# A mixture-of-experts kernel: each expert's result added to the output by two scatters of 512 columns instead of one of 1024

## The chip, the core and the metric

One core of a Trainium2 chip. The time is the device time of one launch in microseconds (us), as the median of several runs. Engines are called by the profile's names: PE (TensorE), PEld (its weight loads), DVE (VectorE), ACT (ScalarE), POOL (GpSimd), SP (SyncE, which here only issues loads and stores; its rows read SPq).

## What is computed

One block of a model, in float32, for 512 tokens of width 1024: a normalisation, three mixing branches (dilated attention, a gated recurrence, attention on a memory), an output projection, and then a mixture of experts with 64 experts, of which each token goes to 8. The change lies in the last part:

```python
D_MODEL = 1024
SEQ = 512
N_EXPERTS = 64
TOP_K = 8
EXPERT_HIDDEN = 256

def swiglu(t, w_up, w_down):
    gate, up = split_cols(t @ w_up, (w_down.shape[0], w_down.shape[0]))
    return (jax.nn.silu(gate) * up) @ w_down

# in routed_experts, for each block of rows of one expert e:
        tok = tok_of_slot[slots]
        y = swiglu(u_pad[tok], w_exp_up[e], w_exp_down[e])
        return acc.at[tok].add(y.astype(jnp.float32) * w_of_slot[slots][:, None]), None

# in reference:
        x = x + y.reshape(B, S, D)
```

An expert's weights are 1024 x 512 (up) and 256 x 1024 (down) floats: 3 MB an expert, 192 MB in all. On average 512 x 8 / 64 = 64 tokens go to an expert.

## The kernel before

The front part (projection, branches, router, shared expert) takes the first 600 us and isn't touched. Then the experts run one after another, 64 times the same work on up to 96 rows (`ROWS`). The program is written by hand for each engine, with semaphores between them; nothing is scheduled by a tool, so the order of each engine's instructions is the order of the code.

For expert e:

- SP loads three blocks of 1 MB (two of up, one of down, lines 450 and 452) into 12 buffers, that is, up to four experts ahead. A load waits only for PE to have used the block that lay in its buffer (`block_used`).
- POOL gathers the expert's rows of `u_dram` by the token numbers in `index` (`gather`, line 512), into one of two buffers; 96 descriptors, of which those that hold no token (4096 and above) are skipped by the bounds check. It waits until PE has turned the rows of expert e - 2 (`gT_done`).
- PE turns the rows (`transpose_tokens`, L1786), ACT and DVE split them into a high and a low part (`gatheredT`, L550 and L1346), and so they do with each weight block (ACT `high`, L550, DVE `low`, L1339).
- PE does `up` (24 matmuls of 512 columns) and, after DVE's gate (L1353, L1356) and another turn (L1807), the down product (12 matmuls) into two banks, one for each half of the 1024 columns (all in L1436).
- ACT copies the two banks into `y_out` (`result`), one of two buffers, and raises `y_ready` after the second copy.
- POOL adds the rows of `y_out` to the output in DRAM with an accumulating indirect DMA (`scatter`, line 520). It waits for `y_ready` and for the whole scatter of the expert before (`added`), since two experts may add to the same token's row.

On POOL the order is gather(e + 3), scatter(e), gather(e + 4), scatter(e + 1) and so on; its queue is in order, so that a gather stands behind the scatter before it. On PE it is, for expert n: turn of the hidden rows of n, `up` of n + 1, turn of the gathered rows of n + 2, down of n. Line 501 is `wait_pass`, the helper that waits; `index_ready` comes from DVE (`read_deal`, lines 1333 and 1334), once. A second pass for experts with over 96 tokens is in the program and isn't taken here: the trace has 64 gathers and 64 scatters.

Of the kernel before, what the change touches and what calls it, by code (L numbers as in the profile page):

```python
# [20 lines left out]
U32 = mybir.dt.uint32  # L21
ALU = mybir.AluOpType
# [4 lines left out]
D, T, M = 1024, 512, 256  # L27
# [6 lines left out]
E, FH = 64, 256  # L34
# [8 lines left out]
ROWS = 96  # L43
# [7 lines left out]
NO_TOKEN = 4096.0  # L51
# [50 lines left out]
def build(nc, io, out, const, u_dram, table_dram, debug=None):  # L102
    ctx = ExitStack()
    with ctx:
        def sem(name):
            return ctx.enter_context(nc.semaphore(name))
# [7 lines left out]
        def at(offset, *shape):  # L114
            return view(arena[:, offset:offset + int(np.prod(shape))], *shape)

        def take(*shape):
            offset = top[0]
            top[0] += int(np.prod(shape))
            assert top[0] <= words, top[0]  # L120
            return offset

        square = at(take(6, P), 6, P)
        ident, flip, counting, before, ones, level = (square[:, n, :] for n in range(6))
        index = at(take(E), E).bitcast(U32)
        slot_w = at(take(E), E)
        gains = at(take(32), 32)
        lb = at(take(8), 8)
# [64 lines left out]
        def rounded_pair(name, offsets, *shape):  # L193
# [39 lines left out]
        y_out = at(logits_at, 2, D)  # L233
# [10 lines left out]
        ps = [ctx.enter_context(nc.psum_tensor(f"bank{n}", [P, 512], F32)) for n in range(8)]  # L244
# [34 lines left out]
        place_split, hot_ready, set_done, own_ready, folded, index_ready = map(  # L279
            sem, ("place_split", "hot_ready", "set_done", "own_ready", "folded", "index_ready"))  # L280
# [1 line left out]
        gT_done, gT_high, gT_low = map(sem, ("gT_done", "gT_high", "gT_low"))  # L282
        tanh_done, act_ready, hid_ready, hidT_done, hidT_high, hidT_low = map(
            sem, ("tanh_done", "act_ready", "hid_ready", "hidT_done", "hidT_high", "hidT_low"))
        y_ready, added = map(sem, ("y_ready", "added"))

# [189 lines left out]
        @block.gpsimd  # L478
        def _(pool):
            pool.memset(eps, EPS).then_inc(c_in[8], 1)  # L480
            pool.wait_ge(c_in[8], 1)
            pool.memset(rel[32:33, :], 1.0).then_inc(c_in[8], 1)
            for n, name in enumerate(("q_norm_a", "k_norm_a", "q_norm_c", "k_norm_c")):
                for half in range(2):
                    pool.dma_start(gain_rows[16 + n:17 + n, half * HD:(half + 1) * HD], io[name]).then_inc(c_in[1], 16)
            pool.dma_start(rel[0:32, :], io["rel_bias"]).then_inc(c_in[5], 16)
            pool.dma_start(bucket[0:33, :], const["bucket"]).then_inc(c_in[6], 16)
            pool.dma_start(out_norm, bcast(io["out_norm_b"], P, BV)).then_inc(c_in[7], 16)


            bound = pool.to_reg(T - 1)
            out_rows = out.rearrange("a t d -> (a t) d")

            turn = pool.alloc_register("passes_done")
            target = pool.alloc_register("wait_value")

            def wait_pass(semaphore, r, scale, plus):


                if isinstance(r, int):  # L500
                    pool.wait_ge(semaphore, plus)
                else:
                    pool.reg_mul(target, turn, scale)
                    pool.reg_add(target, target, plus)
                    pool.wait_ge(index_ready, 1)
                    pool.wait_ge(semaphore, target)

            def gather(e, r):

                if e >= 2:  # L510
                    wait_pass(gT_done, r, E, e - 1)
                pool.indirect_dma_start(gathered[0:ROWS, e % 2, :], None, u_dram,  # L512
                                        bass.IndirectOffsetOnAxis(ap=index[0:ROWS, e:e + 1], axis=0),
                                        bounds_check=bound, oob_is_err=False).then_inc(gather_in[e % 2], 16)

            def scatter(e, r):
                wait_pass(y_ready, r, E, e + 1)
                if not isinstance(r, int) or e >= 1:
                    wait_pass(added, r, 16 * E, 16 * e)
                pool.indirect_dma_start(out_rows, bass.IndirectOffsetOnAxis(ap=index[0:ROWS, e:e + 1], axis=0),  # L520
                                        y_out[0:ROWS, e % 2, :], None, bounds_check=bound, oob_is_err=False,
                                        compute_op=ALU.add).then_inc(added, 16)

            def expert_pass(r):
                wait_pass(index_ready, r, 1, 1)
                for e in range(3):
                    gather(e, r)
                for e in range(E):
                    if e + 3 < E:
                        gather(e + 3, r)  # L530
                    if isinstance(r, int) and e == 0:
                        pool.wait_ge(out_stored, 16 * NT)
                    scatter(e, r)
                wait_pass(added, r, 16 * E, 16 * E)

            pool.wait_ge(u_stored, 16 * NT)
            expert_pass(0)
            pool.reg_mov(turn, 0)
            fullest = pool.value_load(most_i[0:1, 0:1], min_val=0, max_val=T)
            with pool.If(fullest > ROWS):  # L540
                with pool.Fori(1, PASSES) as r:
                    with pool.If(fullest > r * ROWS):
                        pool.reg_add(turn, turn, 1)
                        expert_pass(r)
# [3 lines left out]
        def _(act):  # L548
            def copy(o, i, **kw):
                return nc.scalar.activation(o, i, ACT.Copy, **kw)  # L550
# [251 lines left out]
            def result(n, m, used):  # L802

                act.wait_ge(block_used, used)
                if not isinstance(m, int) or m >= 2:
                    act.wait_ge(added, m * 16 - 16)
                copy(y_out[0:ROWS, n % 2, 0:512], ps[4][0:ROWS, :])
                copy(y_out[0:ROWS, n % 2, 512:1024], ps[6][0:ROWS, :]).then_inc(y_ready, 1)

            def expert(n, m, u, round0, start=False, last=False):  # L810

# [47 lines left out]
        def _(dve):  # L859
            v = nc.vector  # L860
# [119 lines left out]
            for g in range(1, len(groups)):  # L980
# [3 lines left out]
                if g <= 2:  # L984

                    a, name = ((qa, "qa"), (ka, "ka"))[g - 1]
# [341 lines left out]
            def read_deal(r):  # L1328

                dve.wait_ge(folded, r + 1)  # L1330
                if not isinstance(r, int):
                    dve.wait_ge(added, r * (16 * E))
                v.tensor_reduce(slot_w[0:ROWS, :], ps[7][0:ROWS, E:3 * E].rearrange("p (v e) -> p e v", v=2), AX.X, ALU.add)
                v.tensor_scalar(index[0:ROWS, :], ps[7][0:ROWS, 0:E], NO_TOKEN, None, ALU.add).then_inc(index_ready, 1)  # L1334

            def low(q, u):

# [91 lines left out]
        def _(pe):  # L1429
# [57 lines left out]
            n = 0  # L1487
# [270 lines left out]
            def deal_sets(r):  # L1758


                pe.wait_ge(hot_ready, r * 2 + 2)
                if isinstance(r, int):
                    pe.wait_ge(s_hidT_out, 2)
                else:
                    pe.wait_ge(y_ready, r * E)
                for g in range(SETS):
                    bank, c0 = set_bank(g)
                    for t in range(NT):
                        last = mm(bank[:, c0:c0 + 144], lo_hot[:, t, PER * g:PER * (g + 1), :].rearrange("p e s -> p (e s)"),
                                  hi_hot[t // 2][:, t % 2 * SETS + g].rearrange("p k e -> p (k e)"), start=t == 0, stop=t == NT - 1)  # L1770
                last.then_inc(set_done, 1)
# [30 lines left out]
            def expert(n, m, u, turn, last_turn=False):  # L1802


                pe.wait_ge(hid_ready, m + 1)
                for f in range(2):
                    last = tr(ps[3][:, f * ROWS:(f + 1) * ROWS], hid[0:ROWS, n % 2, f * P:(f + 1) * P], ident[0:ROWS, 0:ROWS])  # L1807
                last.then_inc(hidT_done, 1)
                if not last_turn or n + 1 < TURN:
                    up(n + 1, m + 1, u + BLOCKS)  # L1810
                if not last_turn or n + 2 < TURN:
                    transpose_tokens(n + 2, m + 2, turn + (n + 2) // 2)
                pe.wait_ge(low_done, u + 3)
                pe.wait_ge(hidT_low, m + 1)
                if not isinstance(m, int) or m >= 1:
                    pe.wait_ge(y_ready, m)
                both = [high_part[(BLOCKS * n + 2) % HIGHS], low_part[(BLOCKS * n + 2) % SLOTS]]
                for half in range(2):
                    for f in range(2):
                        last = products(ps[4 + 2 * half][0:ROWS, :], [hidT[:, n % 2, part, f * ROWS:(f + 1) * ROWS] for part in range(2)],  # L1820
                                        [part[:, 2 * f + half, :] for part in both], f == 0, f == 1)
                last.then_inc(block_used, 1)
# [55 lines left out]
```

## Time and profile before

| | us |
|---|---|
| median of 3 runs | 1245.78 (1243.4 to 1246.14) |
| the profiled execution | 1241.29 |
| its span (first to last instruction) | 1239.1 |
| of it PE busy | 1139.6 (92%) |
| DVE busy | 901.4 (73%) |
| ACT busy | 720.9 (58%) |
| POOL busy | 244.7 (20%) |

Read it so: the span is 2.2 us under the time of the same execution, and that execution is 4.5 us under the median, so that differences are to be taken within one profile and put on the median afterwards. The DMA engines have no row among the engines; their share stands in the 40 slices and in the views of a stretch. A share of the DMA above 1 means that packets overlap on an engine.

### The profile page before, as it was taken

The page shows a single profiled execution, that of the slowest core. Times are in us where ns is not written, and L with a number is a line of the kernel's source. Part 1 is how long each engine was busy: PE and PEld are TensorE (multiplying, and loading weights), DVE is VectorE, ACT ScalarE, POOL GpSimd, SP SyncE. Part 2 cuts the span into 40 slices and gives each one's busy share as a digit, 9 for nine tenths or more (in the row PEclk, how much of TensorE's full clock was granted, in tenths as well). Part 3 has the DMA queues.
Part 4 walks back from the last instruction along what each step waited for, and adds up shares of the span by engine and source line. Part 5 has one row for each costly group of instructions (what it writes and reads, how often), then busy time and mean ns, then how long its engine had stood idle before and what let it go on. Part 6 is the DMA issues. An engine that isn't in the chain of part 4 may idle for free.

```text
span 1239.1 us, 16255 instructions
## 1 busy us (share of the span) xinstructions
PE 1139.6 (92%) x5693; PEld 861.0 (69%) x5693; DVE 901.4 (73%) x1133; ACT 720.9 (58%) x926; POOL 244.7 (20%) x145
## 2 busy tenths in 40 slices
PE   4999998989999899798998999999999999999993
PEld 3699997766677688675666666666666666667662
DVE  4486378545432585676898889898988999999991
ACT  7543343334333422412787777888878888887881
POOL 1000000000000000001133333343334443444321
PEclk9999998999999999998999999999999999999997
DMA  6413222221212323445799999999999999999992
GB/s 211 134 52 102 86 94 68 68 69 34 68 34 68 133 101 102 160 180 219 276 369 359 364 369 378 370 376 369 369 359 355 369 372 366 369 370 370 356 320 32
DMA packets 74495, 285.58 MB, mean 230 GB/s; under 512 B 10868, under 2 KB 33416, under 8 KB 49620
## 3 DMA queue, kind: packets, MB, share of 16 engines
q1 hardware_dynamic: 59716, 251.16, 54.0%
q0 software_dynamic: 14736, 33.87, 11.3%
q8 instruction: 24, 0.39, 0.1%
q14 instruction: 19, 0.16, 0.0%
HBM read 272.39 MB, written 29.38 MB: 244 GB/s over the span
## 4 chain that ended last, share of the span: by engine, by line
PE 46%; DMA 35%; DVE 7%; issue 6%; ACT 4%; POOL 0%; DVEq 0%; SPq 0%; POOLq 0%; ACTq 0%
PE bank L1436 36%; DMA out_dram<-arena 33%; PE bank L1604 2%; PE bank L1631 2%; DVE low L1339 1%; PE bank L1515 1%; ACT arena L550 1%; ACT high L550 1%; PE bank L1749 1%; DMA arena<-u_rows,arena 1%; PE bank L1616 1%; PE bank L1786 1%; DVE arena L1170 1%; DMA arena<-in_x_dram 1%; DVE gatheredT L1346 1%
## 5 line engine op out<-in xcount | busy, mean ns | idle before, releaser
L1339 DVE TENSOR_TENSOR low<-arena,high 128x2048 fp32r<-128x2048 f32 x192 | 434.0, 2288 | 49.8 <-ACT high L550 48.2
L550 ACT ACTIVATE high<-arena 128x2048 fp32r<-128x2048 f32 x192 | 361.0, 1917 | 0.3 <-DMA arena<-in_w_exp_up_dram 0.3
L1436 PE MATMUL bank<-high,gatheredT 128*96 128x512 f32 x1024 | 325.4, 399 | 15.9 <-DVE gatheredT L1346 15.4
L512 POOL DMA_INDIRECT arena<-u_rows,arena x64 | 116.0, 1813 | 603.7 <-DVE arena L1334 572.2
L1436 PEld LDWEIGHTS bank<-high,gatheredT 128*96 128x96 f32 x1024 | 160.9, 162 | 86.7 <-issue 17.6
L1436 PE MATMUL bank<-low,gatheredT 128*96 128x512 f32 x512 | 202.8, 396 | 0.0
L520 POOL DMA_INDIRECT out_dram<-arena x64 | 122.6, 1916 | 375.5 <-DMA out_dram<-arena 247.5
L1436 PE MATMUL bank<-high,hidT 128*96 128x512 f32 x512 | 164.8, 403 | 1.5 <-ACT arena L550 1.5
L1436 PE MATMUL bank<-hT_high,front_split 128*128 128x512 f32 x448 | 145.7, 407 | 0.8 <-DVE hT_low L879 0.8
L550 ACT ACTIVATE arena<-bank 96x512 f32<-96x512 f32 (+4 forms) x217 | 107.6, 533 | 66.6 <-PE bank L1436 29.9
L1436 PEld LDWEIGHTS bank<-low,gatheredT 128*96 128x96 f32 x512 | 82.8, 162 | 36.3
L1436 PEld LDWEIGHTS bank<-hT_high,front_split 128*128 128x128 f32 x448 | 82.4, 191 | 28.5 <-issue 11.5
L1436 PE MATMUL bank<-low,hidT 128*96 128x512 f32 x256 | 101.4, 396 | 0.0
L1436 PEld LDWEIGHTS bank<-high,hidT 128*96 128x96 f32 x512 | 78.4, 163 | 29.1 <-issue 1.6
L873 DVE TENSOR_TENSOR front_split<-arena,front_split 128x2048 fp32r<-128x2048 f32 (+2 forms) x26 | 52.1, 2004 | 60.0 <-ACT front_split L550 60.0
L1436 PE MATMUL bank<-front_split,hT_high 128*128 128x384 f32 (+1 forms) x384 | 94.7, 328 | 0.0
L1436 PE MATMUL bank<-hT_low,front_split 128*128 128x512 f32 x224 | 88.5, 395 | 0.0
L550 ACT ACTIVATE gatheredT<-bank 128x384 fp32r<-128x384 f32 x128 | 55.9, 489 | 39.9 <-PE bank L1786 39.1
L550 ACT ACTIVATE front_split<-arena 128x2048 fp32r<-128x2048 f32 (+2 forms) x36 | 62.6, 1738 | 25.6 <-PE bank L1436 16.7
L1436 PEld LDWEIGHTS bank<-front_split,hT_high 128*128 128x128 f32 x384 | 67.9, 188 | 0.8 <-issue 0.2
L1786 PEld LDWEIGHTS bank<-arena 96*128 96x128 f32 x512 | 48.3, 140 | 27.2 <-DMA arena<-u_rows,arena 18.1
L1346 DVE TENSOR_TENSOR gatheredT<-bank,gatheredT 128x384 fp32r<-128x384 f32 x128 | 64.8, 546 | 2.5 <-ACT gatheredT L550 2.4
(249 smaller groups left out, 1420.7 us busy)
## 6 DMA issues: line engine op xcount, KB each, us to landing
arena<-in_w_exp_up_dram SPq DMA_DIRECT2D x128, 1024.0 KB
arena<-in_w_exp_down_dram SPq DMA_DIRECT2D x64, 1024.0 KB, 7.5
arena<-in_w_in_dram SPq DMA_DIRECT2D x14, 1024.0 KB, 5.3
arena<-in_w_in_dram SPq DMA_DIRECT2D x10, 768.0 KB, 4.5
arena<-in_w_branches_dram SPq DMA_DIRECT2D x4, 1024.0 KB, 5.0
arena<-in_w_out_dram SPq DMA_DIRECT2D x4, 1024.0 KB, 5.1
arena<-in_x_dram SPq DMA_DIRECT2D x4, 512.0 KB, 5.4
arena<-in_w_mem_kv_dram SPq DMA_DIRECT2D x2, 1024.0 KB, 5.2
```

Source lines behind the costliest of these rows:

```text
L512: pool.indirect_dma_start(gathered[0:ROWS, e % 2, :], None, u_dram, bass.IndirectOffsetOnAxis(ap=index[0:ROWS, e:e + 1], axis=0), bounds_c ...
L520: pool.indirect_dma_start(out_rows, bass.IndirectOffsetOnAxis(ap=index[0:ROWS, e:e + 1], axis=0), y_out[0:ROWS, e % 2, :], None, bounds_ch ...
L550: return nc.scalar.activation(o, i, ACT.Copy, **kw)
L873: v.tensor_tensor(low_part, raw_block(w), high_part.bitcast(F32), ALU.subtract).then_inc(front_low, 1)
L1170: v.scalar_tensor_tensor(u_tok[:, t, :].rearrange("p (k f) -> p f k", k=KD), x_tok[:, t, :].rearrange("p (f k) -> p f k", k=KD), small[:, ...
L1339: v.tensor_tensor(low_part[q % SLOTS], raw[q % SLOTS], high_part[q % HIGHS].bitcast(F32), ALU.subtract).then_inc(low_done, 1)
L1346: v.tensor_tensor(parts[:, 1], view(ps[half][:, 0:4 * ROWS], 4, ROWS), parts[:, 0].bitcast(F32), ALU.subtract).then_inc(gT_low, 1)
L1436: ins = mm(bank, left[a], right[b], start=first and q == 0, stop=last and q == 2)
L1515: last = mm(ps[4 + q][:, z * P:(z + 1) * P], left[rows, b, c * P:(c + 1) * P], right[rows, b, c * P:(c + 1) * P], start=True, stop=True)
L1604: mm(ps[2 + j % 2][:, 0:keys], qkT[rows, 0, t * P:(t + 1) * P], qkT[rows, 1, 0:keys], start=True, stop=True).then_inc(qk_done, 1)
L1631: last = mm(ps[j % 2][:, 0:HD], probsT[:, j % 2, kt * P:(kt + 1) * P], values, start=kt == 0, stop=kt == tiles - 1)
L1786: last = tr(ps[k // 4][:, (k % 4) * ROWS:(k % 4 + 1) * ROWS], gathered[0:ROWS, n % 2, k * P:(k + 1) * P], ident[0:ROWS, 0:ROWS])
```

## The change

The result of an expert goes out in two accumulating scatters, one for columns 0 to 511 and one for columns 512 to 1023. The output is seen as 1024 half rows of 512 columns; token t's halves are the half rows 2t and 2t + 1, whose numbers DVE writes once into `half_index`. Each half has its own semaphores: ACT raises `y_ready[h]` after the copy of that half, a scatter of a half waits for that half's copy and for the scatter of the same half of the expert before.

```diff
-            bound = pool.to_reg(T - 1)
-            out_rows = out.rearrange("a t d -> (a t) d")
+            bound, half_bound = pool.to_reg(T - 1), pool.to_reg(2 * T - 1)
+            out_halves = out.rearrange("a t (h d) -> (a t h) d", h=2)
...
-            def scatter(e, r):
-                wait_pass(y_ready, r, E, e + 1)
+            def scatter(e, h, r):
+                wait_pass(y_ready[h], r, E, e + 1)
                 if not isinstance(r, int) or e >= 1:
-                    wait_pass(added, r, 16 * E, 16 * e)
-                pool.indirect_dma_start(out_rows, bass.IndirectOffsetOnAxis(ap=index[0:ROWS, e:e + 1], axis=0),
-                                        y_out[0:ROWS, e % 2, :], None, bounds_check=bound, oob_is_err=False,
-                                        compute_op=ALU.add).then_inc(added, 16)
+                    wait_pass(added[h], r, 16 * E, 16 * e)
+                pool.indirect_dma_start(out_halves, bass.IndirectOffsetOnAxis(ap=half_index[0:ROWS, h, e:e + 1], axis=0),
+                                        y_out[0:ROWS, e % 2, 512 * h:512 * (h + 1)], None, bounds_check=half_bound,
+                                        oob_is_err=False, compute_op=ALU.add).then_inc(added[h], 16)
...
-                    scatter(e, r)
-                wait_pass(added, r, 16 * E, 16 * E)
+                    for h in range(2):
+                        scatter(e, h, r)
+                for h in range(2):
+                    wait_pass(added[h], r, 16 * E, 16 * E)
...
                 act.wait_ge(block_used, used)
-                if not isinstance(m, int) or m >= 2:
-                    act.wait_ge(added, m * 16 - 16)
-                copy(y_out[0:ROWS, n % 2, 0:512], ps[4][0:ROWS, :])
-                copy(y_out[0:ROWS, n % 2, 512:1024], ps[6][0:ROWS, :]).then_inc(y_ready, 1)
+                for h in range(2):
+                    if not isinstance(m, int) or m >= 2:
+                        act.wait_ge(added[h], m * 16 - 16)
+                    copy(y_out[0:ROWS, n % 2, 512 * h:512 * (h + 1)], ps[4 + 2 * h][0:ROWS, :]).then_inc(y_ready[h], 1)
...
-                v.tensor_scalar(index[0:ROWS, :], ps[7][0:ROWS, 0:E], NO_TOKEN, None, ALU.add).then_inc(index_ready, 1)
+                v.tensor_scalar(index[0:ROWS, :], ps[7][0:ROWS, 0:E], NO_TOKEN, None, ALU.add)
+                for h in range(2):
+                    last = v.tensor_scalar(half_index[0:ROWS, h, :], ps[7][0:ROWS, 0:E], 2.0, 2 * NO_TOKEN + h, ALU.mult, ALU.add)
+                last.then_inc(index_ready, 1)
...
-                    pe.wait_ge(y_ready, m)
+                    pe.wait_ge(y_ready[1], m)
```

On POOL, before the change, at the start of the experts (the `out_dram` rows are the scatters, the `u_rows` rows the gathers):

```order
L512 DMA arena<-u_rows,arena 96x1024 [waits gT_done] x2
L520 DMA out_dram<-arena 512x1024 [waits y_ready,out_stored]
L512 DMA arena<-u_rows,arena 96x1024 [waits gT_done]
L520 DMA out_dram<-arena 512x1024 [waits added,y_ready]
L512 DMA arena<-u_rows,arena 96x1024 [waits gT_done]
L520 DMA out_dram<-arena 512x1024 [waits added,y_ready]
```

The same place of the changed kernel:

```order
L514 DMA arena<-u_rows,arena 96x1024 [waits gT_done] x2
L522 DMA out_dram<-arena 1024x512 [waits y_ready0,out_stored]
L522 DMA out_dram<-arena 1024x512 [waits y_ready1]
L514 DMA arena<-u_rows,arena 96x1024 [waits gT_done]
L522 DMA out_dram<-arena 1024x512 [waits added0,y_ready0]
L522 DMA out_dram<-arena 1024x512 [waits added1,y_ready1]
L514 DMA arena<-u_rows,arena 96x1024 [waits gT_done]
L522 DMA out_dram<-arena 1024x512 [waits added0,y_ready0]
```

Each gather now stands behind two scatters in POOL's queue instead of one. All else on POOL keeps its place.

## Rows read from the trace of the kernel before

**Rows 1.** The page: the chain that ended last by engine and line, and the DMA slices.

```profile
PE 46%; DMA 35%; DVE 7%; issue 6%; ACT 4%; POOL 0%; DVEq 0%; SPq 0%; POOLq 0%; ACTq 0%
...
DMA  6413222221212323445799999999999999999992
```

**Rows 2.** The chain in order of time (start, us, what), early in the experts.

```profile
621.56 9.05 DMA out_dram<-arena
...
630.65 0.76 issue
631.41 8.87 DMA out_dram<-arena
```

**Rows 3.** Two stretches: busy us (x instructions) of PE, PEld, DVE, ACT, POOL; PEclk, DMA share, GB/s.

```profile
620.00:930.00 310.00, 293.56 (x1428) 204.50 (x1427) 275.85 (x249) 246.18 (x280) 112.37 (x63) 0.99 1.02 368
...
930.00:1190.00 260.00, 252.73 (x1244) 178.85 (x1243) 239.34 (x216) 215.73 (x244) 108.15 (x55) 1.00 1.02 366
```

**Rows 4.** POOL in order of time: start, us, instruction, [idle before <- what ended it].

```profile
621.56 2.73 POOL L520 DMA_INDIRECT out_dram<-arena  x1 [7.08 <-DMA out_dram<-arena]
...
929.95 1.44 POOL L520 DMA_INDIRECT out_dram<-arena  x1 [6.79 <-ACT arena L550]
...
1180.04 1.44 POOL L520 DMA_INDIRECT out_dram<-arena  x1 [5.67 <-ACT arena L550]
1181.79 2.52 POOL L512 DMA_INDIRECT arena<-u_rows,arena  x1 [0.30 <-issue]
1189.59 1.61 POOL L520 DMA_INDIRECT out_dram<-arena  x1 [5.28 <-DMA out_dram<-arena]
```

**Rows 5.** Who POOL waited for: us, times, longest; 620 to 930, then 930 to 1190.

```profile
POOL out_dram L520 <- DMA out_dram<-arena: 186.9, 31, 7.1
...
POOL out_dram L520 <- ACT arena L550: 100.6, 19, 6.8
POOL out_dram L520 <- DMA out_dram<-arena: 49.8, 9, 6.1
```

**Rows 6.** DMA queues (packets, MB, share of 16 engines) and down loads (landing), 620 to 930.

```profile
q1 hardware_dynamic: 13393, 97.52, 81.0%
q0 software_dynamic: 6949, 16.48, 21.3%
...
arena<-in_w_exp_down_dram SPq DMA_DIRECT2D x31, 1024.0 KB, 7.4
```

**Rows 7.** The down loads' issue to landing from 930 to 1190 (median), from 1100 to 1200.

```profile
arena<-in_w_exp_down_dram SPq DMA_DIRECT2D x27, 1024.0 KB, 11.8
...
DMA to landing us min/median/max: 13.6/14.7/15.8
```

**Rows 8.** ACT in order of time at 1200: the split of an up block.

```profile
1200.55 1.92 ACT L550 ACTIVATE high<-arena 128x2048 fp32r<-128x2048 f32 x1 [0.27 <-DMA arena<-in_w_exp_up_dram]
```

**Rows 9.** The hardware DMA queue from 20 to 100, when it carries short packets.

```profile
q1 hardware_dynamic: 4576, 7.10, 28.5%
```

**Rows 10.** Scatter to landing (min/median/max): 620 to 930, then 930 to 1190; POOL's own times in the first.

```profile
DMA to landing us min/median/max: 8.6/9.2/9.7
...
L520 POOL DMA_INDIRECT out_dram<-arena x32: 1443/2005/3267, 621.6 to 929.9; - x32
...
DMA to landing us min/median/max: 8.1/8.7/9.6
```

**Rows 11.** The last part of the chain in order of time.

```profile
1191.51 11.37 DMA arena<-u_rows,arena
...
1215.77 1.08 ACT arena L550 x2
...
1217.23 5.48 DMA out_dram<-arena
...
1223.54 1.42 POOL out_dram L520
```

**Rows 12.** PEld turning gathered rows, in order of time.

```profile
1193.14 0.87 PEld L1786 LDWEIGHTS bank<-arena 96*128 96x128 f32 x8
1202.92 0.70 PEld L1786 LDWEIGHTS bank<-arena 96*128 96x128 f32 x8 [0.67 <-DMA arena<-u_rows,arena]
```

**Rows 13.** The write of the token numbers (ns), once.

```profile
L1334 DVE TENSOR_SCALAR arena<-bank x1: 211/211/211, 578.2 to 578.2; 96x64 uint32<-96x64 f32 x1
```

More of the change, by code:

```diff
@@ L125, in build @@
         index = at(take(E), E).bitcast(U32)
+        half_index = at(take(2, E), 2, E).bitcast(U32)
         slot_w = at(take(E), E)
@@ L284, in build @@
             sem, ("tanh_done", "act_ready", "hid_ready", "hidT_done", "hidT_high", "hidT_low"))
-        y_ready, added = map(sem, ("y_ready", "added"))
+        y_ready = [sem(f"y_ready{h}") for h in range(2)]
+        added = [sem(f"added{h}") for h in range(2)]
         groups = [("qf", QB, 512), ("qa", QA, AW), ("ka", KA, AW), ("va", VA, AW), ("ib", IB, BV), ("og", OG, BV),
@@ L1331, in read_deal @@
                 if not isinstance(r, int):
-                    dve.wait_ge(added, r * (16 * E))
+                    for h in range(2):
+                        dve.wait_ge(added[h], r * (16 * E))
                 v.tensor_reduce(slot_w[0:ROWS, :], ps[7][0:ROWS, E:3 * E].rearrange("p (v e) -> p e v", v=2), AX.X, ALU.add)
-                v.tensor_scalar(index[0:ROWS, :], ps[7][0:ROWS, 0:E], NO_TOKEN, None, ALU.add).then_inc(index_ready, 1)
+                v.tensor_scalar(index[0:ROWS, :], ps[7][0:ROWS, 0:E], NO_TOKEN, None, ALU.add)
+                for h in range(2):
+                    last = v.tensor_scalar(half_index[0:ROWS, h, :], ps[7][0:ROWS, 0:E], 2.0, 2 * NO_TOKEN + h, ALU.mult, ALU.add)
+                last.then_inc(index_ready, 1)
             def low(q, u):
@@ L1764, in deal_sets @@
                 else:
-                    pe.wait_ge(y_ready, r * E)
+                    pe.wait_ge(y_ready[1], r * E)
                 for g in range(SETS):
```

## The prediction

> **What bounds the kernel now.** I read the page first. Its chain gives a third of the span to DMA, and the slices show the DMA engines nine tenths busy from about 600 us on [rows 1]; so the expert part is the place to look. The chain in order of time then shows the bare wait that the change is after: scatter, 0.8 us of issue, scatter, again and again [rows 2]. Read alone, this says that the scatters set the pace.
>
> The pace comes from POOL in order of time [rows 4]. Scatter 1 starts at 621.56 and scatter 32 at 929.95: 31 experts in 308.4 us, 9.95 us each. Scatter 59 starts at 1189.59: 27 experts in 259.6 us, 9.62 us each. These are two stretches with different releasers: in the first POOL waits for the scatter before 31 times of 32, in the second for ACT's copy 19 times of 28 [rows 5]. In the second PE is 97.2% busy (252.73 of 260), in the first 94.7% [rows 3]. So with the scatter chain out of the way PE would go at about 9.62, and the chain seems to cost 0.33 us an expert in the first stretch.
>
> The third view speaks against that. The DMA share is 1.02 in both stretches, and the rate is 368 and 366 GB/s, the same though PE is 3.5% faster in the second [rows 3]. 368 GB/s over 9.95 us is 3.66 MB an expert; at 366 GB/s that takes 10.0 us. So in the second stretch PE uses up an expert in 9.62 us while the DMA engines bring one in 10.0. The difference has to show in the loads, and it does: from issue to landing a down block takes 7.4 us in the first stretch [rows 6], 11.8 in the second and 14.7 from 1100 to 1200, at most 15.8 [rows 7]. (14.7 - 7.4) over the 23 experts from 930 to 1150 is 0.32 us an expert, near the 0.38 of the rates. The loads run up to four experts ahead, and this cushion is being eaten. At 1200.55 it is gone: ACT waits for an up block of the last expert [rows 8]. The kernel lives on its cushion for 27 experts and it just lasts.
>
> So the bound is the work of the DMA engines, about 10.0 us an expert; the chain of scatters in the first stretch is a follower, since each scatter shares engines that are full.
>
> **The change, part by part.**
>
> *The chain gets looser: worth nothing in the end.* A half scatter lands sooner. Bounds: not below 5.4 us, what a whole scatter takes in the empty tail (5.48, [rows 11]), not above the 9.2 of a whole one beside the loads [rows 10]; I take 8. With the 0.8 us of issue that is 8.8, under 9.62, so the wait for the scatter before goes. If nothing else bound, the first stretch would fall from 9.95 to 9.62: 31 x 0.33 = 10.2 us, at most 11 with the start. But then PE outruns the DMA from the start, by 0.38 us an expert. The cushion is what was eaten in the second stretch, about 27 x 0.38 = 10 us, gone after some 27 experts; from then on PE waits for weights at 10.0 us an expert. The last block lands when the DMA engines have done their work, and that is when it lands now. Credit: 0.
>
> *Twice as many accumulating packets: the cost.* A row of 4 KB becomes two of 2 KB. Some 64 more data packets an expert are 4 more on each of 16 engines. No row shows such a packet, so I bound its overhead from two rows of the other queue. Short packets: 28.5% of 16 engines over 80 us is 365 us, over 4576 packets 80 ns each, of 1552 bytes [rows 9]. Long ones: 81.0% of 16 engines over 310 us is 4018 us, over 13393 packets 300 ns each, of 7281 bytes [rows 6]. A straight line through both gives 38 ns for 1000 bytes and 20 ns for the packet itself. Low end: nothing, if an addition's cost goes with bytes alone. Middle: 20 ns a packet, 4 x 20 = 0.08 us an expert. High end: the addition reads twice and writes once, 3 x 20 ns each, 0.24 us. To that come the small packets of a second scatter: 32 skipped rows and 16 completions, 3 an engine, at 0 to 20 ns, 0 to 0.06 us. I take 0.08 + 0.03 = 0.11 us an expert; bounds 0 and 0.30. Since nothing hides DMA work here, times 64: 7.0 us, bounds 0 and 19.
>
> *POOL issues 64 more scatters.* Each takes 1.44 us alone and 2.0 in the median of the first stretch, up to 3.27 [rows 10]; with 0.3 us between them [rows 4]. POOL is a third busy, so it is no bound. But gather(e + 4) stands behind them. Now it starts 1.75 us after the scatter (1181.79 after 1180.04, [rows 4]). Afterwards the first half starts half of ACT's 1.08 us earlier [rows 11], and one more scatter and gap come in: -0.54 + 1.7 to 2.3 = 1.2 to 1.8 us later. PE turns these rows 11.35 us after the gather's start (1193.14 against 1181.79, [rows 4, 12]) and didn't wait; the next gather, issued at 1191.51, took 11.37 and was waited for, 0.67 us [rows 11, 12]. In the first stretch the gather is behind a late scatter and will come earlier. At 10 us an expert PE comes 0.4 us later for each expert that lies between, which takes up part of it. I book 0 here and keep the rest as a rival.
>
> The GPSIMD Engine Reference of the Trainium skill (in its table of the engine's properties, the row on SBUF interfaces) says that POOL shares them with DVE and contends with DVE instructions that have two SBUF inputs, as `low` has. By that rule the third issue in a row would meet `low` more often; the spread of 1.44 to 3.27 us agrees with it [rows 10].
>
> *DVE writes two more index tables before `index_ready`:* 2 x 0.21 us, once [rows 13]. The gathers start 0.4 us later; 0 to 0.4, I take 0.2.
>
> *ACT* has one more wait in `result`, for a semaphore that was raised long before: two experts back, 0.
>
> *The tail.* Scatter 62 starts at 1217.23 and lands after 5.48, scatter 63 starts at 1223.54 [rows 11]. Afterwards each half's chain is as long but for some bytes; the second half starts 1.2 us later, for 0.3 to 0.6 us less transfer twice. 0, within 1 us either way.
>
> **The sum**, against the profiled execution: 1241.3 + 7.0 + 0.2 = 1248.5. It lay 4.5 us under the median of the runs shown; on the median that is 1253.0.
>
> The Trainium skill, DMA: Bandwidth & Descriptors, section "Why small descriptors are slow (HBM only)", gives a fixed overhead of about 3 beats of 32 bytes a packet. By this page alone a 2 KB packet costs some 2% more for its bytes and the whole change about 2 us (an estimate from that page), which would be no difference that can be told. No row here shows an accumulating half row, so the bounds above stay as they are.
>
> **The rivals.**
>
> *B. The bytes alone count.* The DMA engines bound, and a half row costs half: the overheads are 0. Then only the 0.2 us is left: 1246. For it: the line of 20 ns is drawn through two mixes of transfers, and stalls in either may have made it. Against: such overhead can hardly be 0.
>
> *C, the other side. The wait for the scatter before is a real bound, and the DMA engines have room.* Place: the first stretch. Price: 31 x 0.33 = 10 us less, 1235.5. For it: the chain [rows 2], and 31 waits of 32 [rows 5]. Against: the share of 1.02 and the growing landing times [rows 3, 7]. It decides if the DMA engines can bring an expert in under 9.8 us; then the cushion lasts to the end even at PE's pace.
>
> *D. The gather is late.* If the gather starts 1.8 us later and takes 10 to 11.4 us as before, it lands up to 1.5 us after PE wants it. The delay turns around a loop of two experts (gather, turn, down, copy, scatter, gather), so PE goes at 9.62 + 0.75 = 10.4 against 10.1: 0.3 us x 60 = 18 us beyond the 7, and 1271 at worst; half of it, 1262, is the likelier. It decides when the gather lands later than about 13.9 us after the first copy's scatter started. For it: the gather waits at the end [rows 12]. Against: 27 experts at 9.62 without such a wait, and room of 0.4 us an expert from the slower pace.
>
> **How the numbers follow.** What a measurement of this kernel can tell from no change is about 0.2%, 2.5 us. Forecast (DMA-bound, dearer halves, 2.5 to 16 us more): 0.45. B: 0.22. C: 0.15. D: 0.18. Slower is 0.45 + 0.18 = 0.63, same 0.22, faster 0.15. The range goes from 1241, which leaves out most of C, to 1268, which leaves out the top of D; about 0.17 lies outside.
>
> **What the profile after would show.** The DMA share stays at 1.0 or above from 620 us until the last weights; 128 scatters; POOL's waits on the scatter before shrink from 236 us to a small part, and ACT's copies take their place from the start. The experts go at about 9.6 us until some 900 us and at 10.1 after that, and ACT's `high` waits for up blocks there, by some 10 to 15 us in all. If instead the share falls to 0.98 and the last experts still go at 9.6, C was right. If PE waits for gathers in the second half, D was. If the landing of the loads stays flat at 7.4 us with experts of over 10.0 us, some wait that I haven't named has taken over. The prediction is wrong most simply if a half row's addition costs the engines far more than 60 ns over its bytes.

## The result, and the profile after

The changed kernel is slower: a median of 1266.07 us in five executions against 1245.78 before (1240.28 to 1248.77, 5), ratio 1.0154 with a 95% interval of 1.0124 to 1.0184, that is about 19 us. Four of the five lie between 1260.55 and 1267.03 (median 1263.61); the fifth, 1746.61, ran at a mean granted PE clock of 0.61 of full speed instead of 0.98, and all ratios here leave out executions that took over 1.5% more than the fastest of their kernel. The profile below is that of another execution of the same kernel. Timed again in the first series of experiments the changed kernel gave 1266.38 against 1245.46, 21 us more.

The page of the changed kernel: the chain by engine and by line, the DMA slices, and POOL's DMA queue (packets, MB, share of 16 engines).

```profile
PE 47%; DMA 29%; POOL 7%; issue 6%; DVE 6%; ACT 3%; SPq 0%; ACTq 0%; DVEq 0%; POOLq 0%
PE bank L1444 36%; DMA arena<-u_rows,arena 17%; DMA out_dram<-arena 11%; POOL out_dram L522 7%; PE bank L1794 2%; PE bank L1612 2%; PE bank L1639 2%; ACT arena L554 1%; PE bank L1523 1%; PE bank L1757 1%; PE bank L1624 1%; DVE arena L1174 1%; DMA arena<-in_x_dram 1%; DVE low L1347 1%; DVE arena L975 0%
...
DMA  6322241212121332736899999999999999999972
...
q0 software_dynamic: 21904, 33.89, 12.1%
```

In [rows 1] DMA had 35% of the chain; scatters alone were 33%. Now it is 29%, the gathers (`u_rows`) are the largest part of it, and POOL, which had 0%, has 7%. The queue carries 7168 packets more than the 14736 of before, for the same bytes. The two stretches of [rows 3] again:

```profile
620.00:930.00 310.00, 285.29 (x1387) 197.14 (x1386) 268.45 (x241) 239.51 (x271) 183.99 (x92) 1.00 1.03 354
930.00:1190.00 260.00, 241.29 (x1174) 167.45 (x1172) 226.11 (x204) 201.80 (x229) 157.97 (x77) 0.99 1.03 357
```

PE is less busy in both (92.0% and 92.8%, from 94.7% and 97.2%). The DMA share is no lower than before, 1.03 from 1.02, and yet it stands for 354 and 357 GB/s instead of 368 and 366. The waits of [rows 5] and their neighbours, 620 to 930 and then 930 to 1190 (us, times, longest):

```profile
POOL out_dram L522 <- ACT arena L554: 84.7, 28, 4.5
...
PEld bank L1794 <- DMA arena<-u_rows,arena: 32.5, 27, 2.2
POOL out_dram L522 <- DMA out_dram<-arena: 30.9, 20, 3.6
...
PE bank L1794 <- DMA arena<-u_rows,arena: 20.7, 23, 1.7
...
PEld bank L1794 <- DMA arena<-u_rows,arena: 22.5, 19, 2.4
POOL out_dram L522 <- DMA out_dram<-arena: 22.1, 14, 2.7
```

The wait that the change is after went, from 236.7 us to 53.0. In its place PE waits for gathered rows. All turns of gathered rows, in the changed kernel and then in the one before: count, first and last start; the waits of PEld and PE for gathers added up (us, times); and, from the gathers' own view, who waited for them:

```profile
L1794 PEld LDWEIGHTS bank<-arena x512: 137/140/145, 583.2 to 1231.1; 96*128 96x128 f32 x171
...
  DMA arena<-u_rows,arena: 98.5, 88
...
  PEld bank L1794: 59.8, 49
  PE bank L1794: 38.6, 39
```

```profile
L1786 PEld LDWEIGHTS bank<-arena x512: 137/140/145, 585.9 to 1203.5; 96*128 96x128 f32 x171
...
  DMA arena<-u_rows,arena: 28.6, 30
...
  PEld bank L1786: 18.1, 17
  PE bank L1786: 10.5, 13
```

PE's waits are in turns in which PEld waits too, at the same time, so the sum counts most late gathers twice. By PEld alone 49 of the 64 turns were late in the changed kernel, 59.8 us in all, and 17 turns, 18.1 us, before. The rows also give the pace: from the first turn to the last, 63 experts on, it takes 647.9 us instead of 617.6, 10.28 us an expert instead of 9.80. The spans differ by 1263.7 - 1239.1 = 24.6, and that is these 30.3, less 2.7 by which the experts began earlier and 3.0 by which the tail was shorter.

Why the gather is late stands in POOL in order of time (start, us, instruction, [idle before <- what ended it]). The changed kernel, and then the one before at the same place:

```profile
1063.22 2.27 POOL L522 DMA_INDIRECT out_dram<-arena  x1 [2.81 <-ACT arena L554]
1065.79 3.06 POOL L522 DMA_INDIRECT out_dram<-arena  x1 [0.31 <-issue]
1069.15 1.48 POOL L514 DMA_INDIRECT arena<-u_rows,arena  x1 [0.30 <-issue]
```

```profile
1064.23 1.80 POOL L520 DMA_INDIRECT out_dram<-arena  x1 [5.22 <-ACT arena L550]
1066.33 2.60 POOL L512 DMA_INDIRECT arena<-u_rows,arena  x1 [0.30 <-issue]
```

The gather started 2.10 us after the scatter and now starts 5.93 us after the first of the two. Over the 60 gathers that stand right behind scatters it is 2.25 us in the mean before and 5.84 now: 2.25 for the first issue, 0.88 until the second begins, 2.40 for the second, 0.30 until the gather. From that follows a loop, which the chain of the changed kernel shows whole (start, us, what):

```profile
1167.66 9.81 DMA arena<-u_rows,arena
1177.47 0.04 issue
1177.52 0.88 PE bank L1794 x8
1178.40 2.78 PE bank L1444 x12
...
1181.61 0.60 ACT arena L554
...
1182.47 1.31 POOL out_dram L522
1183.79 1.27 issue
1185.05 3.05 POOL out_dram L522
1188.10 0.30 issue
1188.41 9.94 DMA arena<-u_rows,arena
```

Gather, turn, down product, ACT's copy, two scatters' issue on POOL, gather: 1188.41 - 1167.66 = 20.75 us for two experts, 10.4 each. The stretch on POOL in it is 5.9 us. With the 2.1 of before in its place, the whole of ACT's copy (0.5 more) and the 11.4 us that the gather took before [rows 11] instead of 9.8 it would be 20.75 - 3.8 + 0.5 + 1.6 = 19.0 us, just under the 19.6 of two experts before. This is an estimate: 11.4 is the landing of the only gather on that kernel's chain.

### The profile page after: what moved, and what is told of

Same layout as the page of the kernel before. It is cut to its first block, busy times and chain, and to the rows that moved or that the text cites. A ratio compares the mean times of both kernels' runs of the same rounds, so it can differ in the third digit from the quotient of the medians.

```text
span 1744.8 us, 16386 instructions
## 1 busy us (share of the span) xinstructions
PE 1692.4 (97%) x5693; PEld 1047.0 (60%) x5693; DVE 913.6 (52%) x1135; ACT 723.0 (41%) x926; POOL 301.6 (17%) x209
## 4 chain that ended last, share of the span: by engine, by line
PE 49%; DMA 29%; issue 19%; DVE 1%; ACT 1%; POOL 0%; POOLq 0%; SPq 0%; DVEq 0%
PE bank L1444 38%; DMA out_dram<-arena 28%; PE bank L1612 2%; PE bank L1639 2%; PE bank L1523 2%; PE bank L1757 1%; PE bank L1624 1%; PE bank L1545 1%; PE bank L1602 0%; POOL out_dram L522 0%; DMA arena<-in_x_dram 0%; PE bank L1657 0%; PE bank L1777 0%; ACT arena L554 0%; PE bank L1453 0%
## 5 line engine op out<-in xcount | busy, mean ns | idle before, releaser
L1444 PE MATMUL bank<-high,gatheredT 128*96 128x512 f32 x1024 | 437.8, 519 | 2.4 <-DVE gatheredT L1354 2.4
L522 POOL DMA_INDIRECT out_dram<-arena x128 | 186.9, 1460 | 528.4 <-ACT arena L554 505.6
L1444 PE MATMUL bank<-low,gatheredT 128*96 128x512 f32 x512 | 263.1, 514 | 0.0
L1444 PE MATMUL bank<-high,hidT 128*96 128x512 f32 x512 | 221.1, 523 | 1.5 <-ACT arena L554 1.5
L1444 PE MATMUL bank<-hT_high,front_split 128*128 128x512 f32 x448 | 218.1, 586 | 0.0
L1444 PE MATMUL bank<-front_split,hT_high 128*128 128x384 f32 (+1 forms) x384 | 142.4, 464 | 0.0
L1444 PE MATMUL bank<-low,hidT 128*96 128x512 f32 x256 | 131.3, 513 | 0.0
L1444 PE MATMUL bank<-hT_low,front_split 128*128 128x512 f32 x224 | 128.7, 575 | 0.0
L803 ACT ACTIVATE arena<-bank 96x256 f32<-96x256 f32 x64 | 24.4, 381 | 200.5 <-PE bank L1444 200.5
L1444 PE MATMUL bank<-front_split,hT_low 128*128 128x384 f32 (+1 forms) x192 | 88.6, 461 | 0.0
```

What stands on the lines that cost most here:

```text
L522: pool.indirect_dma_start(out_halves, bass.IndirectOffsetOnAxis(ap=half_index[0:ROWS, h, e:e + 1], axis=0), y_out[0:ROWS, e % 2, 512 * h:5 ...
L803: nc.scalar.activation(e_tanh[0:ROWS, n % 2, :], ps[2 + 3 * (n % 2)][0:ROWS, 0:FH], ACT.Tanh, scale=0.5).then_inc(tanh_done, 1)
L1444: ins = mm(bank, left[a], right[b], start=first and q == 0, stop=last and q == 2)
```

## The experiments

Two explanations were to be told apart, and a third question was open. The late gather: POOL's time for a second scatter, whatever it carries. The data: twice the packets on DMA engines that are full. And what the finer wait is worth. All medians are in us with their range and number of runs; the ratio is to the kernel before on the same chip, with its 95% interval. "Pace" is that of the turns in us an expert, as above, from one profile. The kernel before was timed in each series; its pace is that of the one profile shown.

| kernel | median (range, runs) | ratio | pace |
|---|---|---|---|
| before, series 1, 2, 3 | 1245.46, 1244.18, 1245.63 | 1 | 9.80 |
| changed kernel again | 1266.38 (1262.02 to 1271.7, 6) | 1.0173 (1.0146 to 1.0201) | 10.28 |
| changed, gather in front | 1239.51 (1237.15 to 1244.47, 8) | 0.9958 (0.9939 to 0.9977) | 9.83 |
| the same, series 3 | 1241.71 (1238.7 to 1244.94, 12) | 0.9972 (0.9954 to 0.9991) | 9.84 |
| changed, gather between | 1243.76 (1235.55 to 1269.27, 12) | 0.9999 (0.9972 to 1.0026) | 9.79 |
| before, gather in front | 1241.44 (1238.49 to 1251.62, 12) | 0.9976 (0.9955 to 0.9996) | 9.76 |
| before + null scatter behind | 1256.79 (1248.88 to 1262.5, 6) | 1.0103 (1.006 to 1.0147) | 10.13 |
| before + null scatter in idle time | 1246.49 (1240.61 to 1252.85, 12) | 1.0007 (0.9982 to 1.0033) | 9.87 |
| halves chained | 1292.63 (1286.61 to 1299.59, 6) | 1.0378 (1.0341 to 1.0414) | 10.72 |
| halves chained, gather in front | 1288.16 (1286.31 to 1294.07, 5) | 1.0358 (1.0329 to 1.0386) | 10.55 |
| before + extra copies | 1274.04 (1261.88 to 1278.89, 4) | 1.0238 (1.0172 to 1.0305) | 10.24 |
| no scatter | 1211.07 (1208.94 to 1212.32, 4) | 0.9742 (0.9699 to 0.9786) | 9.57 |

### The changed kernel again

> The changed kernel once more, for a profile at full clock and a second set of times. Theory 1 (the DMA engines bound and half rows are dearer): share of DMA 1.0 or above from 620 us on, landing of the down blocks grows, ACT waits 10 us and more for up blocks late in the experts, time 1260 to 1267. Theory 2 (the gathers are late, since they stand behind two scatters on POOL): the share of DMA falls below that of before (under 1.0), PE's turns of gathered rows (L1794) wait for gathers some tens of us in all, ACT waits for no block.

1266.38, and the profile of the section above: the result repeats. ACT waits for no block and PE waits for gathers, as the second theory had it. Its other sign, a DMA share under 1.0, didn't come: the share is 1.03, and what fell is the rate.

### The changed kernel with the gather in front of both scatters

```diff
-                for e in range(3):
+                for e in range(4):
                     gather(e, r)
                 for e in range(E):
-                    if e + 3 < E:
-                        gather(e + 3, r)
+                    if e + 4 < E:
+                        gather(e + 4, r)
```

Four gathers go out at the start, and gather(e + 4) then stands in front of the scatters of e, so it no longer waits for them.

> The changed kernel with each gather one step earlier on POOL: gather(e + 4) stands before both scatters of e instead of behind them. Same DMA work. Theory 1 (DMA work bounds): 1260 to 1267, no change to the changed kernel. Theory 2 (late gathers): 1240 to 1250, the 20 us come back.

> The changed kernel with its gather first, a second time on another chip or day: 1237 to 1244, 0.2 to 0.6% under the kernel before.

1239.51 and 1241.71: all 20 us come back and 4 to 6 more with them. In neither profile does PE wait for a gather. What is waited for now are the loads, and the scatter before (first of the two profiles, 930 to 1190):

```profile
POOL out_dram L522 <- DMA out_dram<-arena: 60.8, 34, 3.7
ACT high L554 <- DMA arena<-in_w_exp_up_dram: 24.3, 30, 2.0
```

Here the DMA engines are the limit, in the way the prediction had it for the change: ACT waits for blocks. In the changed kernel ACT's split waits for no block at all. This shows that the place of the gather is what makes the change dear.

### The kernel before with the gather one step earlier

The same edit on the kernel before (three gathers become four, `e + 3` becomes `e + 4`).

> The kernel before with each gather one step earlier on POOL, in front of the scatter. Theory 1 (DMA work bounds): within 3 us of before. Theory 2 (the scatter wait holds up the gather and with it PE in the first stretch): 8 to 11 us faster, about 1236.

1241.44, 3 us by the ratio, 4 by the medians: nearer to the "within 3 us" than to the 1236 that a gain from the first stretch would have made. The change on top of it takes off 2 us or nothing (1239.51, 1241.71): with the gather out of the way two half scatters cost and bring nothing that could be told. ACT waits for blocks here too, 20.9 us in 27 waits from 930 to 1190.

### The gather between the two scatters

```diff
                 for e in range(E):
-                    if e + 3 < E:
-                        gather(e + 3, r)
...
-                    for h in range(2):
-                        scatter(e, h, r)
+                    scatter(e, 0, r)
+                    if e + 4 < E:
+                        gather(e + 4, r)
+                    scatter(e, 1, r)
```

(with four gathers at the start). The gather stands behind one scatter, as in the kernel before, and all the data of the change is there.

> The changed kernel with gather(e + 4) between the two half scatters of e: one scatter ahead of it, as before the change. Theory 2: the gather comes about as late as before the change, 1240 to 1248. Theory 1: 1260 to 1267.

1243.76, no difference from before that can be told. In its profile the gather starts 2.77 us after the first half's scatter, and PE waits for no gather:

```profile
1064.76 2.46 POOL L522 DMA_INDIRECT out_dram<-arena  x1 [1.74 <-ACT arena L554]
1067.53 2.44 POOL L514 DMA_INDIRECT arena<-u_rows,arena  x1 [0.31 <-issue]
1070.45 2.30 POOL L522 DMA_INDIRECT out_dram<-arena  x1 [0.48 <-issue]
```

One POOL issue fewer ahead of the gather takes the 20 us away, and the packets are all still there (though half of them now come behind the gather). The times fall in two groups: nine executions from 1235.55 to 1248.68, and three, which the ratio leaves out, of 1263.52, 1264.03 and 1269.27, the time of the changed kernel, at the same granted clock (0.98). None of the three was profiled. In neither series of the gather in front did an execution take over 1244.94.

### A scatter that carries nothing

```diff
                 pool.indirect_dma_start(out_rows, bass.IndirectOffsetOnAxis(ap=index[0:ROWS, e:e + 1], axis=0),
                                         y_out[0:ROWS, e % 2, :], None, bounds_check=bound, oob_is_err=False,
                                         compute_op=ALU.add).then_inc(added, 16)
+                if isinstance(r, int):
+                    pool.indirect_dma_start(out_halves, bass.IndirectOffsetOnAxis(ap=nothing[0:ROWS, e:e + 1], axis=0),
+                                            some, None, bounds_check=half_bound, oob_is_err=False,
+                                            compute_op=ALU.add).then_inc(null_done, 16)
```

The kernel before, and behind each whole scatter one of half rows whose 96 numbers are all out of bounds, so that POOL works and no data moves (`nothing` holds the 96 numbers, `some` is a stretch of SBUF; the queue still carries 112 short packets an expert for it).

> The kernel before with its whole scatter, and behind each a second scatter of half rows whose 96 descriptors are all skipped by the bounds check: POOL's time for one more scatter, and no data. Theory 2 (the gather is late because POOL issues two scatters ahead of it): most of the 20 us appear, 1256 to 1268. Theory 1 (the data of the halves is dear to the DMA engines): within 4 us of before.

1256.79, 12.6 us more. POOL's time in order (L524 is the scatter, L528 the null scatter, L516 the gather):

```profile
1066.48 1.80 POOL L524 DMA_INDIRECT out_dram<-arena  x1 [2.91 <-ACT arena L560]
1068.58 3.04 POOL L528 DMA_INDIRECT out_dram<-arena  x1 [0.30 <-issue]
1071.93 1.49 POOL L516 DMA_INDIRECT arena<-u_rows,arena  x1 [0.30 <-issue]
```

Skipping 96 rows takes POOL as long as sending them, 3.04 us here, and the gather starts 5.45 us after the scatter (5.20 in the mean). By PEld 49 turns wait for gathers again, 52.3 us in all. Then the same null scatter in front of POOL's wait for ACT's copy, where POOL has nothing else to do (there L528 is the scatter and L522 the null one):

> The kernel before with the same skipped half-row scatter as in the run with one behind each scatter, but issued before POOL's wait for the copy, where POOL is idle: the same extra descriptors and POOL time, off the gather's path. If only the place of POOL's time counts, the same as before the change, 1242 to 1248. If the skipped descriptors themselves cost, 1250 to 1257.

```profile
1066.43 1.42 POOL L528 DMA_INDIRECT out_dram<-arena  x1 [3.21 <-DMA out_dram<-arena]
1068.16 2.08 POOL L516 DMA_INDIRECT arena<-u_rows,arena  x1 [0.30 <-issue]
1070.54 2.33 POOL L522 DMA_INDIRECT out_dram<-arena  x1 [0.30 <-issue]
```

1246.49: nothing. The instruction is the same and there are as many; only what stands behind it differs. So it is neither POOL's total time nor the small packets of a null scatter, but the delay of the gather, and this alone is 12.6 of the 20 us (7.5 to 18.3 by the interval).

### The finer wait taken back

```diff
                 if not isinstance(r, int) or e >= 1:
-                    wait_pass(added[h], r, 16 * E, 16 * e)
+                    for k in range(2):
+                        wait_pass(added[k], r, 16 * E, 16 * e)
```

Two scatters, but the first waits for both halves of the expert before.

> The changed kernel, but the first half's scatter waits for both halves of the expert before, as the whole scatter did. Two scatters stay, the finer wait goes. Theory 1 (DMA work bounds): 1260 to 1267, as the changed kernel, since the wait was worth nothing. Theory 2 (late gathers): slower than the changed kernel by 10 us or more, since the gather now stands behind the later wait and two issues.

Here `k` runs over the two halves. 1292.63, 26 us over the changed kernel. Whether this is the late gather once more was tried with the gather in front of both scatters:

> Two scatters, the first of which waits for both halves of the expert before (no finer wait), with the gather in front of both. Against the changed kernel with its gather first (1239.5) only the finer wait is taken away. If the scatter wait is worth nothing while the DMA engines bound, 1239 to 1244. If it is worth something, 1246 to 1255, and the halves' dearer packets, some 7 us, are what it paid for.

1288.16, far outside both ranges that were expected. Moving the gather, which gives the changed kernel 26.9 us, gives 4.5 here (2.5 by the ratios, and their intervals overlap), so that the loss isn't the late gather's and what the expectations say of it as the cause is not borne out. PEld's waits for gathers fall from 61.0 us to 15.2 and the time nearly stays. What holds it is the chain itself. With the gather in front, who waited from 930 to 1190, and a piece of the chain in order of time:

```profile
POOL out_dram L523 <- DMA out_dram<-arena: 71.6, 20, 5.0
...
ACT arena L555 <- DMA out_dram<-arena: 21.2, 30, 2.2
```

```profile
1000.17 1.44 POOL out_dram L523
1001.61 0.30 issue
1001.91 7.16 DMA out_dram<-arena
...
1009.87 1.95 POOL out_dram L523
1011.82 0.30 issue
1012.12 7.44 DMA out_dram<-arena
```

The second half is issued 1.7 us and more after the first, lands later by that, and the first of the next expert waits for it: an expert every 10.55 us. So the finer wait is needed as soon as there are two scatters, and is worth 26 us then, and 46 with the gather in front (1288.16 against 1241.71); it pays for the chain that the second scatter makes longer, and for little beyond.

### How full the DMA engines are

To the kernel before, a copy of 256 KB from DRAM to DRAM is added for each of 60 experts, on SP's queue, and nobody waits for it before the end:

```diff
                     load_expert(g * TURN + n, n, g * (BLOCKS * TURN) + BLOCKS * n)
+                    sp.dma_start(scratch[:, one(g * TURN + n), :], dn_src[:, g * TURN + n, 0:512]).then_inc(extra_done, 16)
```

> The kernel before, with a copy of 256 KB from DRAM to DRAM behind each expert's loads for 60 experts, that nobody waits for until the end: 7% more DMA work and nothing else. If the DMA engines bound the kernel before, 60 x 0.65 to 0.8 us come on top: 1280 to 1295. If they have room, under 1255.

1274.04, about 30 us, between the two expectations: less than the 36 to 51 that full engines would have made, more than the 11 that engines with room would have. It is 0.50 us an expert, for 7% more bytes (0.26 on 3.66 MB). The stretch from 930 to 1190:

```profile
930.00:1190.00 260.00, 241.76 (x1169) 166.82 (x1168) 225.12 (x202) 203.45 (x228) 110.60 (x51) 1.00 1.03 381
```

ACT waits 49.4 us for up blocks from 620 to 1190, in the kernel before 0.3 us in all, so the DMA engines set the pace here. But they move 381 GB/s, with the same share of 1.03 that stood beside 368 and 354. At 381 GB/s the 3.66 MB of before would take 9.6 us, not 10.0 (an estimate: the added copies are part of the 381). From the other side, the kernel before without any scatter (the routed results are left out of the output):

> The kernel before without any scatter (the routed experts' results are left out of the output) and so with gathers that wait for nothing but their buffer. Against the kernel before with its gather first (1241), this takes away 1.3 us an expert of DMA work and the last scatters of some 10 us. If the DMA engines bound with 10.0 us an expert, PE becomes the bound at 9.3 to 9.6: 1200 to 1215. If the DMA engines aren't the bound there, only the tail goes: 1230.

```profile
930.00:1190.00 260.00, 254.60 (x1247) 180.31 (x1246) 238.70 (x218) 215.84 (x244) 39.96 (x26) 1.00 0.89 335
```

1211.07, PE 97.9% busy at 9.57 us an expert with a DMA share of 0.89. That is PE's own pace. The kernel before goes at 9.80, so there is 0.23 us an expert between them, 14.5 in all; by the profiles 16.7 more come from the tail, in which no scatter is left to wait for (from the last turn to the end 18.9 us instead of 35.6), and 1.2 from the start.

## Why the prediction was right or wrong

**The side and the likeliest mechanism.** Slower was right, and 1266 lies in the range of 1241 to 1268, near its top. But the change costs 19 to 21 us where the sum had 7.2, and the mechanism that the forecast of 1253 stood on is not the one that ran. It was rival D, for which the prediction had 1262 to 1271 and a chance of 0.18. That the time lies in the range is luck as far as the forecast's mechanism goes: forecast and D happen to lie on the same side, and the range was drawn wide enough for most of D.

**The step that failed: "I book 0 here and keep the rest as a rival".** The gather behind the second scatter was put at 1.2 to 1.8 us later. At the place shown it is 5.93 - 2.10 = 3.8 us later against the scatter, less the half of ACT's copy by which the first scatter starts earlier, 0.54: 3.3. In the mean it is 5.84 - 2.25 = 3.6, less 0.54: 3.0. Three things make up the difference. The second issue takes 2.40 us in the mean, where I had the 1.4 to 2.0 of a scatter that stands first. It begins 0.88 us after the first has ended, where I had a gap of 0.3: the loop above has 1.27 there, and no row of the kernel before could show a wait that only a second scatter has. And the first issue itself takes 2.25 instead of 1.95. So not the median of all places counts, but the place: at 1065.79 the second in the row takes 3.06 us, with `low` at work on DVE from 1065.26 to 1069.76, and in the kernel before the gather, which had that place, took 2.60. The gather's mean was 1813 ns, and is 1446 ns now that it stands third. The row on SBUF interfaces in the GPSIMD Engine Reference of the Trainium skill (section "Specifications") would have it so. The rows agree with it: the null scatters that lie wholly within `low` took 2.15 to 3.41 us (median 3.05), the two that don't touch it 1.42. But no run took `low` away, so that DVE is the reason stays argued. That the two issues ahead of the gather are the reason is shown: by the null scatter behind (12.6 us) and in idle time (nothing), and by the gather moved in between.

**The room for it.** Against D stood "27 experts at 9.62 without such a wait, and room of 0.4 us an expert". The absence of a wait says nothing of how near it is, and those 27 experts were half of the picture: of the 17 turns of the kernel before that waited for a gather, 16 lie between 620 and 930 (us, times, longest):

```profile
PEld bank L1786 <- DMA arena<-u_rows,arena: 17.4, 16, 2.4
```

For that stretch the prediction named POOL's waits and not PE's. By the loop above the gather had some 0.6 us of room (an estimate), and it came 3.3 us later.

**D's loop**: "gather, turn, down, copy, scatter, gather", two experts long, at 10.4 us, is what the trace shows. The chain has 20.75 us for the two, and the mean over all experts is 10.28.

**The bound: "about 10.0 us an expert".** Half right. The DMA engines do come next: with the gather out of the way ACT waits for blocks and the time stays at 1240. But 10.0 was too high, as 381 GB/s and the paces of 9.76 to 9.84 with ACT waiting for blocks show; a share of 1.02 was read as full. In the changed kernel the DMA engines were not the bound at all: ACT waits for no block, and the rate fell by 2.5 to 4% at a share of 1.03 instead of 1.02.

**"The chain gets looser: worth nothing in the end."** Right in effect, and not for the reason given: with the late gather the DMA engines never became the bound that was to take the gain back. The waits of POOL for the scatter before fell by 184 us and the kernel was none the faster; where the gather is in front, the change brings 0 to 2 us over the gather's own 3 to 4. A half scatter was to land after 8 us; the only profile of two scatters that records many landings (halves chained) has 6.9 and 7.0 in the median of the two stretches. Rival C's 10 us are not there. The finer wait is no luxury all the same, since without it the two scatters make a chain of 10.5 to 10.7 us an expert.

**The dearer packets, 7.0 us.** Not shown. With the gather in front, half rows and whole rows take the same time within 2 us (1239.51 and 1241.71 against 1241.44). B's zero fits, and so do the 2 us estimated from the section "Why small descriptors are slow (HBM only)" of DMA: Bandwidth & Descriptors in the Trainium skill; 7 fit badly. The rates in those two profiles are 364 and 368 GB/s for half rows against 366 and 371, 0.5 to 0.8% less, which would be 3 to 5 us of the experts' 620, and the paces (9.83 and 9.84 against 9.76) point the same way by 4 to 5 us. These are one profile each; the medians don't show it.

**The signs.** 128 scatters, a share of 1.03, POOL's waits gone from the scatter to ACT's copies: as foretold, and they would have been so under D as well. Not as foretold: the experts go at 10.28 us in the mean, and at 10.21 from 929.8 to 1185.1 (25 experts), instead of 9.6 and then 10.1, and ACT's wait for blocks is 0 instead of 10 to 15 us. The last sign named, PE waiting for gathers, is the one that appeared, in the first half already.

**Start and tail.** The 0.2 us for the index tables doesn't show: in this profile the first turn is 2.7 us earlier. The tail was 3.0 us shorter, where I had within 1. Over all the profiles with scatters the first turn lies between 582.7 and 592.3 and the tail takes 32.5 to 39.4 us, so single profiles don't settle either.

**What stays open.** The null scatter costs 12.6 us and the change 19 to 21, at about the same delay of the gather (5.20 in the mean, and 5.84 less 0.54). Some 8 us lie between, by the two intervals (7.5 to 18.3, and 18.2 to 25.0) hardly clear of noise. If they are real, they go with what the null scatter lacks, data in the second scatter, and they vanish with the gather in front or between; whether as packets ahead of the gather in POOL's DMA queue or otherwise wasn't tried. Open too is why three executions of the kernel with the gather between took over 1263 us.

**The best version** is the changed kernel with the gather in front, 1239.51 and 1241.71, 0.3 to 0.4% under the kernel before. Nearly as good and simpler is the kernel before with the gather one step earlier (0.24%).

## What to carry to other kernels

On an engine whose queue is in order, the price of one more instruction is the delay of what stands behind it, not its busy time: the same null scatter cost 12.6 us in front of a gather and nothing behind it. Take its duration from the place it will have, beside what runs there, not from the median, and count the wait that it brings with it; and before booking a delay at 0, work out how much room the delayed transfer has before its reader comes. Put prefetches ahead of the instructions that wait for results, as here, where that made a change that lost 20 us one that loses nothing.

## What the runs showed of the hardware

- An indirect DMA of 96 rows costs POOL its issue time even if every row is skipped: null scatters took 2.15 to 3.41 us where they lie wholly within `low`, and 1.42 where they don't touch it.
- The DMA share doesn't tell how full the engines are once it is near 1: 1.03 stood beside 354, 357, 364, 368 and 381 GB/s. Who waits for a load told it.
- Taking out scatters altogether took the share to 0.89 at 335 GB/s, and the gathers then landed after 5.1 us (median), where those that are on the chain, which are late ones, had taken 9.8 to 11.4.
